# Moving loads and steps in the start and the recurrence of a two-block layer kernel

## What is computed

```python
h = rmsnorm(x, norm1_g)
proj = h @ w_in
...
u = u + mu_prev * (u_prev - u) + mu_next * (u_next - u)
...
for d, reverse in enumerate((False, True)):
    w_log = -jax.nn.softplus(-(w_decay0[d] + jnp.tanh(xw) @ w_decay_up[d]).astype(jnp.float32)) - 0.5
    decay = jnp.exp(-jnp.exp(w_log))
    a = jax.nn.sigmoid(a_gate0[d] + xa @ a_gate_up[d])
    kd = heads(k * (1.0 + (a - 1.0) * k_a))
    ...
    wkv = wkv + wkv7_scan(rh, heads(decay), kd, vh, -kk, kk * ah, reverse)
    bonus = bonus + jnp.sum(rh * kd * r_k, axis=-1, keepdims=True) * vh
```

## Time and profile before

| | before |
|---|---|
| runs | 2876.62 us median (2874.69 to 2878.17, 3 runs) |
| span of the profiled execution | 2875.2 us; the page gives no other time for it |
| TensorE matmul busy | 2722.3 us (95%) |
| VectorE busy | 1588.9 us (55%) |
| ScalarE busy | 909.3 us (32%) |
| chain that ended last | TensorE 80%, transfers 8%, VectorE 7%, ScalarE 3% |
| mean granted TensorE clock | 0.984 of full speed |

### The profile page before, as it was taken

The page is one execution under the profiler, slowest core; times in us unless marked ns, Lnnn a source line. Parts: engine busy times, 40 slices in busy tenths (PEclk is TensorE's granted clock), DMA queues, the critical chain, the costliest instruction groups (busy, mean ns, idle before and its releaser), DMA issues.

```text
span 2875.2 us, 46864 instructions
## 1 busy us (share of the span) xinstructions
PE 2722.3 (95%) x20120; PEld 2016.1 (70%) x20120; DVE 1588.9 (55%) x2978; ACT 909.3 (32%) x1528; POOL 136.1 (5%) x236
## 2 busy tenths in 40 slices
PE   7999999998999989899899999999998999999999
PEld 5777877886743333347677778888876777788887
DVE  4675667665553323345676556665456765543443
ACT  5323232316410100023345533223333455333221
POOL 0010101010000000000000000010000000000000
PEclk9999999999999999999999999999999999999999
DMA  4232323245489999973253236664232442233332
GB/s 154 73 117 86 112 87 115 89 161 199 168 357 427 427 425 427 427 307 97 70 112 127 100 95 190 191 192 152 85 87 74 117 129 85 88 102 96 95 96 81
DMA packets 149928, 475.69 MB, mean 165 GB/s; under 512 B 13633, under 2 KB 40881, under 8 KB 137169
## 3 DMA queue, kind: packets, MB, share of 16 engines
q1 hardware_dynamic: 114688, 367.62, 35.8%
q0 software_dynamic: 24944, 86.63, 9.6%
q10 hardware_dynamic: 10080, 18.35, 2.2%
HBM read 451.05 MB, written 21.51 MB: 164 GB/s over the span
## 4 chain that ended last, share of the span: by engine, by line
PE 80%; DMA 8%; DVE 7%; ACT 3%; issue 2%; POOL 0%; SPq 0%; DVEq 0%; ACTq 0%; POOLq 0%
PE psum L154 77%; DMA wslot<-in_w_gate 3%; PE psum L157 3%; DMA wslot<-in_w_up 2%; DVE slot L163 1%; DMA kT<-qk_rows 1%; DMA ring<-in_w_rwkv_out 0%; DVE m_acc L169 0%; DVE halfL L163 0%; DVE X L163 0%; DVE n_ht L169 0%; ACT hH L160 0%; DMA colb<-in_cols 0%; ACT halfH L160 0%; DVE sc__241 L169 0%
## 5 line engine op out<-in xcount | busy, mean ns | idle before, releaser
L163 DVE TENSOR_TENSOR halfL<-ring,halfH 128x1024 fp32r<-128x1024 f32 x302 | 367.9, 1220 | 546.2 <-ACT halfH L160 545.7
L160 ACT ACTIVATE halfH<-ring 128x1024 fp32r<-128x1024 f32 x302 | 317.3, 1053 | 737.5 <-PE psum L154 729.5
L154 PE MATMUL psum<-hH,halfH 128*128 128x512 f32 x1200 | 481.9, 402 | 4.2 <-ACT U L160 2.2
L154 PE MATMUL psum<-hH,halfL 128*128 128x512 f32 x1200 | 468.9, 391 | 0.0
L154 PE MATMUL psum<-hL,halfH 128*128 128x512 f32 x1200 | 468.8, 391 | 0.0
L154 PEld LDWEIGHTS psum<-hH,halfH 128*128 128x128 f32 x1200 | 225.3, 188 | 77.5 <-issue 26.6
L154 PE MATMUL psum<-wslot,XT 128*64 128x512 f32 x1024 | 237.2, 604 | 26.4 <-DMA wslot<-in_w_gate 13.7
L154 PEld LDWEIGHTS psum<-hH,halfL 128*128 128x128 f32 x1200 | 225.7, 188 | 48.4
L154 PEld LDWEIGHTS psum<-hL,halfH 128*128 128x128 f32 x1200 | 225.9, 188 | 43.1
L154 PE MATMUL psum<-halfH,hH 128*128 128x512 f32 (+2 forms) x576 | 222.6, 386 | 23.3 <-DVE ks L163 10.1
L154 PE MATMUL psum<-halfL,hH 128*128 128x512 f32 (+2 forms) x576 | 212.8, 369 | 0.0
(11 more groups left out here) (491 smaller groups left out, 4134.3 us busy)
## 6 DMA issues: line engine op xcount, KB each, us to landing
wslot<-in_w_gate SPq DMA_DIRECT2D x32, 2048.0 KB, 25.5
wslot<-in_w_down SPq DMA_DIRECT2D x32, 2048.0 KB, 25.4
ring<-in_w_in SPq DMA_DIRECT2D x120, 512.0 KB, 3.7
wslot<-in_w_up SPq DMA_DIRECT2D x30, 2048.0 KB, 25.3
ring<-in_w_gu SPq DMA_DIRECT2D x88, 512.0 KB, 3.7
m_in<-in_w_ada POOLq DMA_DIRECT2D x96, 256.0 KB, 3.1
m_in<-in_w_ada POOLq DMA_DIRECT2D x48, 512.0 KB, 4.8
ring<-in_w_down SPq DMA_DIRECT2D x44, 512.0 KB, 3.6
```

The lines of the kernel that those rows point to most:

```text
L154: return self.e.matmul(*a, **k)
L160: return self.e.activation(*a, **k)
L163: return self.e.tensor_tensor(*a, **k)
```

## The change

- The identity (the first 128 columns of con) and colb are loaded first, under the label "consts"; the rest of con comes third, under "masks". TensorE and VectorE wait for "masks" before the first weight tile. VectorE's memsets of eps and U's edges come before the wait for "consts".
- The angles move from behind tile (0, 0) to behind tile (1, 1). ("values", 0) moves from behind tile (3, 3) to behind four of the eight `more()` that follow.
- Dt2 and D2 wait for Dt; only R0a still waits for R0.
- The bonus product moves on VectorE from `rw_bonus` to just behind R1c of direction 0.

```diff
-        after = {(0, 0): [("tables",)],
+        after = {(0, 0): [],
...
-                 (1, 1): [("lora", 0, 0, 0)],
+                 (1, 1): [("tables",), ("lora", 0, 0, 0)],
...
-                 (3, 3): [("prep", 0, d, 7) for d in range(2)] + [("U", 3), ("shift", 8), ("values", 0)] +
-                         [("shift", j) for j in (9, 10, 11)]}
+                 (3, 3): [("prep", 0, d, 7) for d in range(2)] + [("U", 3)] +
+                         [("shift", j) for j in (8, 9, 10, 11)]}
...
-        for _ in range(8):
+        for n in range(8):
             yield from more()
+            if n == 3:
+                yield "values", 0
...
-                pe.wait_ge(*at("ev", pr, d, "R0" if after == "Dt" else after))
+                pe.wait_ge(*at("ev", pr, d, after))
+                if name == "R0a":
+                    pe.wait_ge(*at("ev", pr, d, "R0"))
...
         norm("n1", n1_xn)
+        pe.wait_ge(*at("masks"))
...
                     ve.tensor_tensor(o, b, piece(d, add), AD).then_inc(*up(D, "ev", pr, d, name))
+                if (name, d) == ("R1c", 0):
+                    ve.wait_ge(*now(D))
+                    ve.wait_ge(*now("rw_dve1"))
+                    ve.tensor_tensor(s["t1"], US[:, pr, :], kds, M).then_inc(*up(R_, "rk2", pr))
 
         def rw_bonus(pr):
-            ve.wait_ge(*at("ev", pr, 0, "W1T"))
-            ve.wait_ge(*at("ev", pr, 1, "W1T"))
-            ve.tensor_tensor(SL[0]["t1"], US[:, pr, :], kds, M).then_inc(*up(R_, "rk2", pr))
...
-        ve.wait_ge(*at("consts"))
         ve.memset(eps, EPS).then_inc(*up("norm_dve", "eps"))
         ve.memset(U[:, :, 0:514:513], 0.0).then_inc(*up(R_))
+        ve.wait_ge(*at("consts"))
...
         ve.tensor_tensor(cact, cact, col("c", 0, 8), M).then_inc(*up("ada_dve", "cact"))
+        ve.wait_ge(*at("masks"))
...
-        po.dma_start(con, T["con"]).then_inc(*landed("consts"))
+        po.dma_start(con[:, 0:128], T["con"][:, 0:128]).then_inc(*landed("consts"))
         po.dma_start(colb, T["cols"]).then_inc(*landed("consts", "consts"))
+        po.dma_start(con[:, 128:NCONS], T["con"][:, 128:NCONS]).then_inc(*landed("masks", "masks"))
```

## The result

The changed kernel takes 2860.6 us (median of four runs, 2858.8 to 2861.6) against 2875.8 in the same job: a ratio of 0.9944 with a 95% interval of 0.9932 to 0.9957, 12 to 20 us less. The forecast was 2859.6 in a range of 2853 to 2869. The span of the profiled execution goes from 2875.2 to 2857.0 us, 18.2 less. The same kernel, run again beside later experiments (e9), has 0.9945 (0.9931 to 0.9958) and a span of 2859.6.

A forecast was written before the change was run, and what follows sets the result against it. The prediction took TensorE, nearly always busy after its first matmul block, as the bound, with gaps of 0.4 to 3.7 us left. Terms -1.5 + 2.2 + 4.9 + 10.7 + 0.7 = 17.0 us; 2876.6 - 17.0 = 2859.6, range 2853 to 2869.

The forecast's parts named there:

- Term A: The start: first matmul 0.7 us sooner, but slow first matmuls cost 2.2, so 1.5 us lost.
- Term B: The angles moved behind tile (1,1): TensorE's 2.25 us wait at U goes, 2.2 us saved.
- Term C: First turned values: 2.0 us of the 3.28 gap and the slow stretch behind it go, 4.9 us saved.
- Term D: Bonus product made earlier: TensorE's waits in four pairs and slow stretches behind them go, 10.7 us saved.
- the fourth rival: TensorE's first block starts at the lower clock and stays there, for 100 us in its example: slower, 2907; chance 0.04.
- Term E: Block powers: Dt2 no longer waits for R0, the gap moves one step, 0.7 us saved of 0 to 2.1.
- The first: Rival: slow stretches stay because short waits around them are enough; saving 9.3 us, 2867.3; chance 0.13.
- The second: Rival at the start: first weight tile comes earlier, no slow stretch follows; saving 22.6 us, 2854.0; chance 0.10.
- The third: Rival: VectorE becomes the recurrence's bound and gives back the block-power and bonus savings; 2871.0, no change; chance 0.08.

The follow-up runs named there:

- e9: The changed kernel again, unchanged, beside e10, e11 and e12: 0.9945, 2861.4 us.
- e6: Changed kernel with 28 more transposes, read by nothing, on TensorE between the first 16 and the first matmul: 0.9927, 2856.8 us.
- e5: Changed kernel with the angles back behind the first weight tile: 0.9966, 2867.5 us.
- e2: Changed kernel with the first turned values back behind the last preparation transposes: 0.9955, 2865.8 us.
- e4: Changed kernel with Dt2 and D2 waiting for R0 again: 0.9942, 2861.8 us.
- e10: Changed kernel with VectorE's two R0 sums behind the two copies of Dt2 instead of ahead of them: 0.9942, 2861.3 us.
- e12: e11 with the modulation step between Dt and R0 moved into the loop of each pair: 0.9934, 2858.4 us.
- e3: Changed kernel with VectorE's product for the bonus back at the end of each pair: 0.9970, 2871.2 us.
- e7: Changed kernel with the rest of con, the lora weights and POOL's other small loads issued only after the first weight tile landed: 0.9917, 2852.0 us.
- e11: Changed kernel with the late loads of e7 and the later R0 of e10: 0.9915, 2852.7 us.
- e1: Changed kernel with its start as before, one load of the constants and eps behind them: 0.9939, 2861.0 us.
- e8: Changed kernel with three of the 24 modulation steps of pair 0 moved into the pair's loop: 0.9939, 2859.3 us.

## Why the prediction was right

**The time** (2859.6 against 2860.6) and the sum of 17.0 us hold: 18.2 by the first pair of traces, 15.6 by the second profile, 12 to 20 by the runs.

**Term A**, -1.5: measured -1.7 and -1.3. Both parts were sized well: the first matmul comes 0.5 and 0.6 us sooner (20.60 and 20.51) for 0.7, and the slow steps cost 2.3 and 2.0 (see e6) for 2.2. The argument of the unequal transposes holds. So does the rule of the Trainium skill (TensorE: Matmul & The Clock Gate, Part 1) beside it, that the slow clock is the default and activity releases it: e6 removes the idleness and with it the loss.

**Term B**, 2.2: 2.5, by the rows 28.96 to 48.01 and 30.68 to 47.22. The gap was counted, and a few tenths around it not. That no slow stretch stood behind the 2.25 was luck of the one trace; e5 shows the other outcome, 4.2. The lora sigmoid slipped, and TensorE did not wait for it.

**Term C**, 4.9: 4.5. The gap of 1.28 ahead of the woven tile (1.2 foretold) and the upper clock behind it are there, and e2 undoes it for 4.4.

**Term D**, 10.7: 6.75 in pair 0 for 6.7 (rows of before and e9 from KV on), 3.0 in pair 1 for 2.9, 0.4 and 1.0 in pairs 2 and 3. The 0.2 charged for the product's new place in pair 2 is not seen. The largest term was the most exact, because each slow stretch was read in the rows behind its gap. One reading was short: the stretch of pair 0 runs from 209.97 to about 217, some 7 us, where the fourth rival takes 6 for the longest; the sum does not use it.

**Term E**, 0.7 of 0 to 2.1: pair 1 gives 2.05 in the first profile and 0.55 in e9, and pair 3 another 0.5 in both (1.05 becomes 0.55, where at most 0.4 was allowed), so 2.5 and 1.0; the bound of 2.1 is passed in the first. Against it stands what e4 saw in pair 0. The gap moved by one step in every pair, as said. How far the term reaches is decided by the slow stretch in pair 1: nine profiles have a wait of 2.03 or 2.04 at that place, and in seven the slow stretch follows. In the three with 1.04 or less (e10 to e12) it does not.

**Not in the sum.** In pair 0 VectorE's waits for modulation loads hold TensorE for 2.0 us (0.71 and 1.30) where before it was 0.26; in the table, 5.3 + 6.75 - 1.75 = 10.3. It was no rival either: the one about VectorE spoke of its work, not of transfers that its queue waits for. In all profiles with the moved powers and unmoved modulation steps the loss is 1.5 to 3.2 us, in e4 0.71; this points at the moved powers, but one profile does not settle it. Against it stand 2.7 us in pair 2 (1.5 in e9): the KV product waited 1.80 before with a slow stretch behind, and 0.43 without one in the first profile (1.67 without one in e9). The slow stretch near 480 takes 1.5 of that back in the first profile (18.5 ahead at the bonus of pair 2, 17.0 ahead at the gap of 1.13 in the loop, 517.47 before and 500.45 after) and is absent in e9. So what was left out nearly cancels. That the total comes within 1.4 us of the 17.0 is therefore in part luck.

**The rivals.** The first (slow stretches stay) falls by e2 and e3 for the two long gaps: with the gap the stretch comes and goes. Its reason, that short waits are enough, is not wrong everywhere: the stretch near 480 stands behind 0.52 us, and against it the prediction had only one gap of 0.44 without one. The second is the one that was argued wrongly. It fell for this change, as the tile still landed at 17.4. But "data moves without a pause until about 20 us, whatever the order" was taken as a bound on what order can do, and e7 shows that it is none: the engines move 407 to 421 GB/s from 4 to 10 us in the changed kernel, and which transfer waits within that is free to choose, if one is held back and not only put behind others on its queue. The rule in the Trainium skill (DMA: Bandwidth & Descriptors, Issuing engines are not separate DMA queues), that transfers of all issuers run on the same 16 engines and interleave, agrees with this too: loads on POOL's queue held up one on SyncE's for 6.7 us. The third (VectorE gives back D and E) did not come for D; for E the waits of pair 0 come close to it (see e4). The fourth (a slow level for over 50 us) did not: the first stretch ended after 5 us.

## What to carry to other kernels

A long gap on TensorE should be priced with the slow matmuls behind it: here 3.28 us cost 6.2 (0.9 for the small and 2.0 for the nine large matmuls) and 3.70 cost 6.7. Before a load is made early, ask what it shares the transfers with: delaying some 1.8 MB that was not needed for 20 us brought the first weight tile 6.7 us sooner and the second transposes 6.1 to 6.5, of which 4.4 were left at the bonus of pair 3 (the ratio fell by 0.0027). At its place that is more than four of the five edits of this change. And take a second profile before a term of one or two microseconds is believed, since the same program differs by as much from run to run at places that only transfers and the clock decide.

## What the runs showed of the hardware

- The granted clock in the profile does not show every slow stretch. In e9 it is 1.00 from 20 to 25 us, while 128x512 matmuls start 0.43 us apart, the same spacing as at 0.50 in the first profile. The length of a step is the safer reading.
- Whether a given gap slows TensorE is not fixed. A gap of 2.25 at U did in e5 and did not before; one of 2.04 in pair 1 did in seven of nine profiles; the first block behind 1.01 or 1.02 us of idleness and 16 transposes was slow in e11 and e12 and not in e1 and e7. Gaps of 3.28 and 3.70 were followed by a slow stretch each time they stood there (before, e2, e3), and so were those of 2.65 and 2.99 in pair 1 (before, e4) and of 4.96 to 5.51 at the start (eight profiles).
- The length of the last gap alone does not decide. The KV product of pair 2 was slow behind 1.80 us before, and fast behind 2.07 in e7 and 2.19 in e8. The gap of 0.52 ahead of the lora product near 480 was followed by a slow stretch in six of fourteen profiles (after, e1, e3, e5, e8, e12), and the same gap behind the bonus of pair 0 in two (e3, e11). In e2, e4, e6 and e10 the stretch comes near 500 instead, behind 1.13 and 0.33 us. Each costs 1.4 to 1.5 us. What else decides was not tested.
- A modulation load of 256 KB, issued beside the same weight tile, lands within 4.1 us of its issue in one run (449.55, used at 453.64) and after 5.3 in another (450.58, used at 455.89).
